# A fourth group of seven products in the down projection of plain gated layers, and the second weight sum of down groups as an accumulating transfer

## The reference

```python
def swiglu(x, w_gate, w_up, w_down):
    return (jax.nn.silu(x @ w_gate) * (x @ w_up)) @ w_down
...
        h = rmsnorm(x, g_ffn1_pre[i])
        x = x + 0.5 * rmsnorm(swiglu(h, w1_gate[i], w1_up[i], w1_down[i]), g_ffn1_post[i])
...
        gate_h = causal_dwconv(up[..., :D_FF_2], ffn_conv_w[l], ffn_conv_b[l])
        hid = jax.nn.gelu(gate_h) * up[..., D_FF_2:]
        x = x + rms_norm(hid @ w_down[l], g_ffn_post[l])
```

## Time and profile before

| | us |
|---|---|
| median of three runs | 2737.84 |
| lowest and highest | 2737.75, 2740.96 |
| the profiled execution | 2738.5 |
| its span, first to last instruction | 2736.6 |
| TensorE busy | 2727.2 |
| VectorE busy | 2058.6 |
| ScalarE busy | 1623.5 |

### The profile page before, as it was taken

One profiled execution on the slowest core, in us unless ns is written; L12 is line 12 of the kernel. 1 busy time (PEld: TensorE's weight loads), 2 busy tenths in 40 slices (PEclk: granted clock), 3 DMA queues, 4 the chain that ended last, 5 costly groups with the idle time before them and its releaser, 6 DMA issues.

```text
span 2736.6 us, 46133 instructions
## 1 busy us (share of the span) xinstructions
PE 2727.2 (100%) x18546; PEld 2488.6 (91%) x18546; DVE 2058.6 (75%) x2754; ACT 1623.5 (59%) x2519; POOL 142.1 (5%) x160
## 2 busy tenths in 40 slices
PE   9999999999999999999999999999999999999999
PEld 8999987599999999999976799999987889999998
DVE  7778766767687787787757587787876746989968
ACT  6556644665566685565626565566754546666665
POOL 0000000000000000000000000000001100000000
PEclk9999999999999999999999999999999999999999
DMA  7776614037776327775331247765233323777651
GB/s 220 180 196 174 178 55 101 17 101 185 190 211 162 103 84 206 178 213 158 93 92 49 93 131 178 207 164 169 78 97 92 93 77 101 181 194 203 153 179 55
DMA packets 177139, 382.55 MB, mean 140 GB/s; under 512 B 35616, under 2 KB 80032, under 8 KB 176928
## 3 DMA queue, kind: packets, MB, share of 16 engines
q1 hardware_dynamic: 159216, 315.63, 37.1%
q0 software_dynamic: 17568, 63.97, 13.7%
q10 hardware_dynamic: 144, 0.00, 0.0%
HBM read 364.87 MB, written 12.58 MB: 138 GB/s over the span
## 4 chain that ended last, share of the span: by engine, by line
PE 99%; DVE 0%; DMA 0%; issue 0%; ACT 0%; SPq 0%; DVEq 0%
PE banks L742 31%; PE banks L743 31%; PE banks L744 31%; PE banks L1292 1%; PE banks L1314 1%; PE banks L1351 1%; PE banks L1303 1%; PE banks L1355 0%; PE banks L1341 0%; PE banks L781 0%; PE banks L1445 0%; DVE PT L3179 0%; PE banks L1274 0%; PE banks L1238 0%; DMA X<-in_x 0%
## 5 line engine op out<-in xcount | busy, mean ns | idle before, releaser
L742 PE MATMUL banks<-HH,WH 128*128 128x256 f32 (+1 forms) x3244 | 1015.8, 313 | 0.6 <-DVE HL L2284 0.4
L743 PE MATMUL banks<-HH,WL 128*128 128x256 f32 (+1 forms) x3244 | 1010.9, 312 | 0.0
L744 PE MATMUL banks<-HL,WH 128*128 128x256 f32 (+1 forms) x3244 | 1010.7, 312 | 0.0
L742 PEld LDWEIGHTS banks<-HH,WH 128*128 128x128 f32 x3244 | 619.1, 191 | 43.6 <-issue 8.3
L743 PEld LDWEIGHTS banks<-HH,WL 128*128 128x128 f32 x3244 | 619.2, 191 | 34.7 <-issue 1.0
L744 PEld LDWEIGHTS banks<-HL,WH 128*128 128x128 f32 x3244 | 619.1, 191 | 34.1
L588 DVE TENSOR_TENSOR WL<-raw,WH 128x1024 fp32r<-128x1024 f32 (+1 forms) x308 | 370.5, 1205 | 215.6 <-ACT WH L583 214.4
L583 ACT ACTIVATE WH<-raw 128x1024 fp32r<-128x1024 f32 (+1 forms) x308 | 319.3, 1040 | 291.7 <-DVE raw L2527 121.9
L742 PE MATMUL banks<-SH,WH 128*128 128x256 f32 x1472 | 416.7, 283 | 0.8 <-issue 0.8
L743 PE MATMUL banks<-SH,WL 128*128 128x256 f32 x1472 | 416.6, 283 | 0.0
L744 PE MATMUL banks<-SL,WH 128*128 128x256 f32 x1472 | 416.6, 283 | 0.0
(11 more groups left out here) (341 smaller groups left out, 3666.8 us busy)
## 6 DMA issues: line engine op xcount, KB each, us to landing
extra_raw<-in_w_quarters SPq DMA_DIRECT2D x96, 512.0 KB, 4.3
raw<-in_w_quarters SPq DMA_DIRECT2D x48, 512.0 KB, 4.8
raw<-in_w_in SPq DMA_DIRECT2D x46, 512.0 KB, 3.7
spare_raw<-in_w_quarters SPq DMA_DIRECT2D x36, 512.0 KB, 4.1
extra_raw<-in_w_quarters POOLq DMA_DIRECT2D x36, 512.0 KB, 7.4
raw<-in_w_down SPq DMA_DIRECT2D x30, 512.0 KB, 3.7
extra_raw<-in_last_quarters SPq DMA_DIRECT2D x26, 512.0 KB, 4.3
raw<-in_w_quarters POOLq DMA_DIRECT2D x24, 512.0 KB, 6.0
```

The source lines that it names most:

```text
L742: e.matmul(o, wh, ah, start=start, stop=False, skip_group_check=skip)
L743: e.matmul(o, wl, ah, start=False, stop=False, skip_group_check=skip)
L744: return e.matmul(o, wh, al, start=False, stop=stop, skip_group_check=skip)
```

## The change

Only for plain stages (`four_down`): three of the four early units go, and a fourth down group takes their place. Down group 11 now has rows 0 to 7 as before; the one early unit has rows 8 and 9 times the first half of the columns; and group 14 multiplies the other six of the rows 8 to 15 by that half, so its products have three weight blocks instead of four (`first`): 18 matmuls each. Its result is added to the early banks; while it runs, ScalarE puts the seeds of the other half back. The stretch between gate group 10 and down group 11 gets an order of its own (`scalar_short_rows`, `vector_short_rows`), with hidden and row sums handled in another order, some of them in group 10, 11 and 12.

For all down groups, of stage 9 too, VectorE's weight sum for product 6 goes: GpSimd's queue gets an accumulating transfer ("fourth") of quarter (1, 0), which waits for the low split of product 2; the next group's sum transfer waits until it has landed.

```diff
+def four_down(s):
+    return s < 9
+def early_units(s):
+    return 1 if four_down(s) else 4
 def seven_groups(s):
-    return range(2, gated_groups(s) + 3)
+    return range(2, gated_groups(s) + 3 + four_down(s))
...
-            if q == "b21":
+            if q == "b21" and g < gated_groups(s):
                 return vec.at("weight_sum", s, g, 6)
-            return low.at(W[s, "seven", g, {"b11": 0, "third": 4, "b22": 5, "sum": 6}[q]])
+            return low.at(W[s, "seven", g, {"b11": 0, "b21": 3, "third": 4, "b22": 5, "sum": 6}[q]])
...
                 if ph in (1, 4):
                     e.wait_ge(*added[SPLIT_OF[ph]].at(s, g))
+                elif ph == 6 and g in down_groups(s):
+                    e.wait_ge(*added["sum"].at("fourth", s, g))
...
-                if key == W[s, "down", DOWN_WHOLE]:
+                third, fourth = ((s, n + 3, "sum"), (s, n + 3, "b22")) if four_down(s) else (W[s, "down", DOWN_WHOLE],) * 2
+                if key == third:
                     sync_fetch(e, s, 2)
+                if key == fourth:
                     sync_fetch(e, s, 3)
...
+            first = 1 if g == gated_groups(s) + 3 else 0
...
-                    for kp in range(4):
+                    for kp in range(first, 4):
...
-            for kp in range(4):
+            for kp in range(early_units(s)):
                 u = W[s, "early", kp]
...
+        def scalar_short_rows(e, s):
+            n = gated_groups(s)
+            scalar_c21(e, s, n - 1)
+            scalar_hidden_high(e, s, 4)
+            scalar_hidden_high(e, s, 6)
+            scalar_row_sum_high(e, s, 0)
+            split_high(e, W[s, "seven", n, 2])
+            scalar_row_sum_high(e, s, 1)
+            for k in range(1, DOWN_SEVEN, 2):
+                scalar_hidden_high(e, s, k)
+            scalar_silu_half(e, s, n - 1, 1)
+            scalar_row_sum_high(e, s, 2)
+            scalar_row_sum_high(e, s, 3)
...
+        def scalar_last_down_seven(e, s, g):
+            x, y, z = seven_banks(s, g)
+            split_high(e, W[s, "seven", g, 3])
+            scalar_copy(e, s, g, "p1", 0, x, third(y), seven_free(s, g)[1][0])
+            split_high(e, W[s, "seven", g, 4])
+            scalar_seed(e, s, 0)
+            scalar_copy(e, s, g, "q5", 1, z, Q5C[:], vec.at("c22", s, g - 1))
+            split_high(e, W[s, "seven", g, 5])
+            scalar_copy(e, s, g, "u2", 2, x, place(s, g, 0, 1), vec.at("half_added", s, 0, 1))
+            split_high(e, W[s, "seven", g, 6])
+            scalar_copy(e, s, g, "c11", 3, y, place(s, g, 0, 0), act.at("seed", s, 0))
+            split_high(e, W[s, "down", DOWN_WHOLE])
+            scalar_seed(e, s, 1, act.at("c11", s, g))
+            scalar_copy(e, s, g, "u3", 4, x, place(s, g, 1, 1), vec.at("half_added", s, 1, 1))
+            split_high(e, W[s, "down", DOWN_WHOLE + 1])
+            scalar_hidden_high(e, s, DOWN_WHOLE)
+            scalar_hidden_high(e, s, DOWN_WHOLE + 1)
+            scalar_seed(e, s, 2, vec.at("c12", s, g))
+            scalar_copy(e, s, g, "c21", 6, x, place(s, g, 1, 0), act.at("seed", s, 1))
+            scalar_seed(e, s, 3, act.at("c21", s, g))
...
-            if g not in seven_groups(s):
+            if g not in seven_groups(s) or (ph == 6 and g in down_groups(s)):
                 return
...
+        def vector_short_rows(e, s):
+            n = gated_groups(s)
+            vector_half_scale(e, s, n - 1, 1)
+            vector_weight_sum(e, s, n, 2)
+            vector_hidden_low(e, s, 4)
+            vector_hidden_low(e, s, 6)
+            split_low(e, W[s, "seven", n, 2])
+            vector_row_sum_low(e, s, 0)
+            vector_row_sum(e, s, 3)
+            vector_row_sum_low(e, s, 1)
...
+            if four_down(s):
+                vector_hidden_low(e, s, 10)
+                vector_hidden_low(e, s, 12)
+                vector_hidden_low(e, s, 14)
             split_low(e, W[s, "seven", g + 1, 2])
...
+        def vector_third_of_four(e, s, g):
...
+            split_low(e, W[s, "seven", g + 1, 1])
+            vector_c22(e, s, g)
+            vector_half_add(e, s, g, 1, 1)
+            vector_weight_sum(e, s, g + 1, 2)
+            vector_c12(e, s, g)
+            vector_half_add(e, s, g, 0, 1)
+            split_low(e, W[s, "seven", g + 1, 2])
+        def vector_fourth_of_four(e, s, g):
...
+            split_low(e, W[s, "down", DOWN_WHOLE])
+            vector_add(e, s, g, 0, 0)
+            vector_c22(e, s, g)
+            vector_add(e, s, g, 1, 1)
+            split_low(e, W[s, "down", DOWN_WHOLE + 1])
+            vector_hidden_low(e, s, DOWN_WHOLE)
+            vector_hidden_low(e, s, DOWN_WHOLE + 1)
+            vector_c12(e, s, g)
+            vector_add(e, s, g, 0, 1)
+            vector_add(e, s, g, 1, 0)
...
+                if g in down_groups(s):
+                    e.wait_ge(*low.at(W[s, "seven", g, 2]))
+                    e.wait_ge(*added["sum"].at(s, g))
+                    e.dma_start(raw_quarter(s, g, "sum")[:], W.quarter(s, g, (1, 0)), accum_op=ALU.add).then_inc(
+                        *added["sum"].done(("fourth", s, g)))
```

More of the change, by code:

```diff
@@ L561, in tiles_free @@
             if s is not None and STAGES[s] == "ffn":
-                e.wait_ge(*pe.at("unit", W[s, "seven", seven_groups(s)[-1 - (tile_of[u] == NSPLIT + 1)], 6]))
+                g = gated_groups(s) + 1 if tile_of[u] == NSPLIT + 1 else seven_groups(s)[-1]
+                e.wait_ge(*pe.at("unit", W[s, "seven", g, 6]))
             elif s is not None and STAGES[s] == "mix":
@@ L678, in sync_sums @@
                 park_at = ((s, 10, "b11"), (s, 10, "b22"),
-                           *(((s, 11, "b11"), (s, 11, "b22")) if n > 11 else (W[s, "early", 0], W[s, "early", 2])))
+                           *(((s, 11, "b11"), (s, 11, "b22")) if n > 11 else (W[s, "early", 0], (s, 11, "sum"))))
                 if key in park_at:
@@ L986, in seven_free @@
                 return group_free(s, g - 2 if g < n else n - 1)[:3]
-            first = [vec.at("evacuated", s, (n - 1) % 2, 3)] if g == n + 1 else [act.at("c21", s, n)]
-            return [first, [act.at("c11", s, g - 1)], [vec.at("c12", s, g - 1)]]
+            first = [vec.at("evacuated", s, (n - 1) % 2, 3)] if g == n + 1 else [act.at("c21", s, g - 2)]
+            second = [vec.at("half_added", s, 0, 0)] if g == n + 3 else [act.at("c11", s, g - 1)]
+            return [first, second, [vec.at("c12", s, g - 1)]]
         def row_sums(tile, i):
@@ L1033, in tensor_seven @@
                         last = trio(e, ps[bank][:, part(up)], high_of(u)[:, c], low_of(u)[:, c], *operand(kp),
-                                    opens and up == kp == 0, kp == 3, not (opens and up == 0))
+                                    opens and up == 0 and kp == first, kp == 3, not (opens and up == 0))
                 last.then_inc(*pe.done(("seven", s, g, ph), ("unit", u)))
@@ L1051, in tensor_ffn @@
             tensor_early_rows(e, s)
-            for g in seven_groups(s)[-3:]:
+            for g in down_groups(s):
                 tensor_seven(e, s, g)
-            added = [[vec.at("quarter_added", s, t, m) for t in range(2)] for m in range(2)]
+            last = n_groups + 3 if four_down(s) else n_groups
+            added = [[vec.at("quarter_added", s, last, t, m) for t in range(2)] for m in range(2)]
             early, late = (list(range(4 * half, 4 * half + 4)) for half in (n_groups % 2, 1 - n_groups % 2))
@@ L1059, in tensor_ffn @@
                              [added[b % 4 // 2] if b in early else [act.at("seed", s, b % 4)] for b in range(DC)],
-                             early + late[2:] + late[:2], False)
+                             late + early if four_down(s) else early + late[2:] + late[:2], False)
         def tensor_early_rows(e, s):
             half, free = gated_groups(s) % 2, group_free(s, gated_groups(s) - 2)
-            for kp in range(4):
+            for kp in range(early_units(s)):
                 u = W[s, "early", kp]
@@ L1669, in after_seven @@
             if g == gated_groups(s) - 1:
-                return W[s, "early", i]
+                return W[s, "early", i] if i < early_units(s) else W[s, "seven", g + 1, i - 1]
             return W[s, "seven", g + 1, i] if g < seven_groups(s)[-1] else W[s, "down", DOWN_WHOLE + i]
@@ L1759, in scalar_seed @@
                 e.wait_ge(*vec.at("half_added", s, t, i // 2))
-            e.wait_ge(*act.at("c21", s, n + 1))
+            for wait in waits:
+                e.wait_ge(*wait)
             e.activation(ps[group_banks(n - 1)[i]][:], C[:, i % 2, i // 2, :], ACT.Copy).then_inc(*act.done(("seed", s, i)))
@@ L1839, in scalar_ffn @@
                     scalar_silu_half(e, s, g, 0)
-            scalar_early_rows(e, s)
-            scalar_down_seven(e, s, n)
-            scalar_down_seven(e, s, n + 1)
-            scalar_down_seven(e, s, n + 2)
+            if four_down(s):
+                scalar_short_rows(e, s)
+            else:
+                scalar_early_rows(e, s)
```

(16 more changed lines are left out.)

120 lines of the change are left out of this document (83 added, 37 removed).

## The result

| | before | after |
|---|---|---|
| median, us | 2737.8 | 2770.9 |
| lowest and highest | 2737.63, 2740.96 | 2768.85, 2772.91 |
| the profiled execution | 2738.5 | 2772.9 |
| its span | 2736.6 | 2770.8 |

The ratio is 1.0118, 95% interval 1.0101 to 1.0136: 33 us slower, where 13 were forecast and 2764 was the end of the range. The direction was right, the size was not.

A forecast was written before the change was run, and what follows sets the result against it. TensorE was taken as the bound. A plain stage: -1.2 + 1.6 + 0 + 1.4 + 1.7 = +3.5 us; four give +14.0, stage 9 gives 0: 2751.8, say 2751, range 2733 to 2764.

The forecast's parts named there:

- The bound and the matmuls: TensorE bounds the kernel, its waits paid in full; fewer matmul us save 1.2 a plain stage, 4.9 in all.
- Group 11, p1: First down group, product 2: TensorE waits 1.6 us a stage for ScalarE's bank copy p1; bounds 1.3 to 2.5.
- Group 13: Low split of (13, 2) done 25.7 us from group 12's start, wanted at 25.9: wait 0, at most 1.8.
- The additions: GpSimd's queue: "fourth" of group 12 takes 7.0 us, group 13's sum 7.6, landing at 15.8; 27 more additions, median above 6.8.
- Group 14's: Last group, products 1 and 2: late sum quarter makes c12 and p1 late, together 1.4 us a stage; bounds 0 to 3.3.
- The down rows': End of the plain stages: waits behind hidden low 16 (0.9) and seeds (0.4 each), 1.7 us a stage.
- Stage 9: Keeps three groups and early rows, with room of over 1 us at each step: 0 us (0 to 2).
- The range: From the bounds, +0.45 a stage gives 2740 and +6.6 gives 2764; stated as 2733 to 2764 us.
- Rival C: Loop of additions closes longer than 20.16 us, over 7.2 each; group 14 waits over 5 a stage: above 2760, chance 0.08.

The follow-up runs named there:

- e9: Changed kernel with "fourth" on its own semaphore behind the next sum addition, hidden lows earlier, copy p1 earlier, last group's hidden splits first: 2737.37 us, ratio 0.9998.
- e11: e9 with ScalarE's row sum highs 2 and 3 back ahead of copy p1, as in the changed kernel: 2745.04 us, ratio 1.0028.
- e1: Changed kernel, four groups kept, with VectorE's weight sum for product 6 back and the transfer "fourth" gone: 2768.6 us, ratio 1.0112.
- e6: Changed kernel with only "fourth" put on its own semaphore and issued behind the next group's sum addition: 2765.41 us, ratio 1.0099.
- e10: e9 with hidden lows 10, 12 and 14 back at the end of VectorE's list for group 12: 2752.54 us, ratio 1.0053.
- e12: e9 with "fourth" back on the sum semaphore, so the next group's sum addition waits until it has landed: 2760.73 us, ratio 1.0085.
- e7: e9 with the last group's and down rows' splits back in the changed kernel's order: 2743.72 us, ratio 1.0023.
- e4: Changed kernel with only ScalarE's row sum highs 2 and 3 moved behind copy p1 of group 11: 2771.16 us, ratio 1.0124.
- e2: Kernel before the change, with only the sum for product 6 of its down groups made by the transfer "fourth": 2738.55 us, ratio 1.0005.
- e8: Changed kernel with VectorE's weight sum back, hidden lows 10, 12, 14 earlier, copy p1 earlier, last group's hidden splits first: 2753.74 us, ratio 1.0057.
- e3: Changed kernel with only hidden lows 10, 12, 14 moved earlier in VectorE's group 12 list and hidden high 14 beside 10 and 12: 2768.11 us, ratio 1.0115.

## Why the prediction was off, by its own steps

**The bound and the matmuls** were right: every us of TensorE's waiting was paid, 216 more matmuls are in the trace, as counted, and with the waits gone (e9) the time is the old one, which fits a saving of 4.9 us less 4.3 of small gaps. By itself such a saving is under what can be told.

**Group 11, p1**: 1.6 predicted, 1.48 measured in each of four stages, 0.27 in a gap behind it, and 7.7 us in all by e11. The chain from row to row held.

**Group 13: the step that failed.** The prediction took product 2 of group 13 as the first that needs what stands at the end of VectorE's list for group 12, and found 25.7 against 25.9, "So 0". But three of the items in that list are hidden lows 10, 12 and 14, and group 13 multiplies hidden rows 8 to 15: its product 0 needs low 10 after three matmuls, 20.5 from the start of group 12, not 25.9. By the prediction's own count low 10 ends 2.3 (two more lows, a split) ahead of 25.7, at 23.4: 2.9 us late in each stage, 11.6 in all, without any other error. The trace bears it out: in each of the four stages the wait is the landing of the sum quarter (19.5, 16.7, 15.4 and 16.4 us into group 12) less 12.9, and the 15.8 that was forecast gives 2.9. In the kernel before those lows were done early because the early units that went had needed them; the cost of their new place was counted as 1.8 us of VectorE's time and not as a deadline.

**The additions.** 7.0 and 7.6 were taken for two in a row, landing at 15.8. That was near in three stages (15.4 to 16.7); in stage 0 it was 7.3 and 10.0, with 1.0 of later issues: 19.5. The longest addition of the earlier trace rows, 9.6, was in the bounds for group 11 and was not carried into this term. And the 5.4 that was read as an addition alone had the DMA engines at a share of 0.73 beside it. The page of the profile counts 27 more additions, as forecast, but with a median of 6.6 us and not above 6.8. The 10.0 explains why the wait is 6.6 in stage 0, against the 2.0 that the order alone makes (e1, e6, e10). By the fit of the Trainium skill (DMA: Bandwidth & Descriptors, Anatomy of one DMA — SWDGE (gpsimd) path) a transfer of 512 KB is estimated at 3.2 us, which would have hidden the chain. No addition here was under 5.1.

**The clock** stood in no term. The earlier trace rows had shown 1.00 throughout, in a program whose longest wait of TensorE was 1.2 us. The Trainium skill (TensorE: Matmul & The Clock Gate, HAM oscillation — how this bites in real kernels) has the mechanism, a wait behind which TensorE restarts throttled; the trace agrees, with 0.50 behind 6.5 us and 0.72 over the six us behind 2.0, though the waits of the page's case are longer than these 2.0. The matmuls behind the four waits took 7.1 us more than at their pitch, of which e10's stage 6 puts 0.6 a stage down to hidden lows 12 and 14 and not to the clock; wherever the prediction had a wait of such a size in its bounds, this belonged beside it.

**Group 14's** 1.4 was not there. Its sum quarter landed 21.9, 18.8, 18.2 and 19.7 us into group 13, where 18.1 was forecast, but group 13 lasted 24.3 to 28.7 in place of 20.16. e12, with shorter waits in group 13, has the forecast wait at product 1 of group 14: 1.2, 3.9, none and 1.1 us. **The down rows'** 1.7 was 1.4 to 2.7, and 6.3 us in e7 against 6.8 predicted. **Stage 9** was put at 0 and became 0.9 shorter.

**The range.** +6.6 a stage is less than the prediction's own upper bounds add up to: -1.2 + 2.5 + 1.8 + 3.3 + 1.7 are 8.1, or 2770. Even so it would have met 2770.9 by luck only, since the waits that the trace has are not those of these bounds.

**Rival C**, the loop that doesn't close, came nearest to 2770.9 in time, but not by its mechanism: it wanted additions of over 7.2 us and waits of over 5 us at group 14. The two of group 12 took 7.35 on average, those behind them 6.0, and group 14 had no wait. e12 shows how much the chain can cost: 23.4 us.

What stays open: why one sum quarter takes 10.0 us in stage 0 and the same step less in others. The window of its flight, of the kernel after:

```profile
268.60:278.60 10.00, 10.00 (x86) 10.00 (x85) 3.06 (x4) 3.05 (x4) 0.86 (x1) 1.00 0.96 288
```

The DMA engines are busy for 0.96 of it, but the same step took 7.6 to 8.0 us in the other stages at shares of 0.93 to 1.00, so the share alone doesn't decide, and no run changed the load on the queues alone. Why e4's additions were the longer ones is open too, and so is what decides whether a wait halves the clock (below).

## What to carry to other kernels

When work is taken away, ask what it had forced to be ready early, and give each operation in a moved list its own deadline: its first reader, not the list's. A transfer that must wait for a landing makes a chain of whole landing times; its own semaphore and a place behind what is urgent were worth 23 us here. The engine time that a transfer saves has no fixed price: nothing with the old lists (e2), 16 us with four groups and full lists (e8 against e9). And test a suspected wait by taking its cure out of the version that has no waits: cured alone in the slow kernel, three causes seemed worth 2.8, -0.3 and 5.5 us (e3, e4, e6); taken out of the fast one, the same three cost 15.2, 7.7 and 23.4.
